# Loading a ring of expert weights in pairs: one 4 MB transfer and one semaphore for two 2 MB units in the middle rounds

## The chip, the cores and the metric

The kernel runs on one core of a Trainium2 chip. The metric is the device time of one execution in microseconds (us). All data are float32.

## The reference, cut to what matters

One decoder layer for 256 tokens of width 1024: two gated token mixers, then a mixture of 32 experts with four experts per token, then a final norm. The mixers, the router and the norms make up the first fifth of the time; the rest is the expert part:

```
def expert_block(args):
    xb, e = args
    gu = xb @ w_gu[e] + b_gu[e]                 # 1024 x 2048
    glu = jnp.minimum(gu[:, :D_FF], SWIGLU_LIMIT)
    lin = jnp.clip(gu[:, D_FF:], -SWIGLU_LIMIT, SWIGLU_LIMIT)
    act = glu * jax.nn.sigmoid(SWIGLU_ALPHA * glu) * (lin + 1.0)
    return act @ w_d[e] + b_d[e]                # 1024 x 1024
```

Each expert's weights (8 MB for gate and up, 4 MB for down) are read from HBM once. With 32 experts that is about 400 of the 432 MB that the kernel moves.

## The kernel before

**Items and rounds.** An *item* is one expert with up to 64 of its tokens; there are 32 items here. Two items (one even, one odd) make a *round*: 16 rounds, numbered 0 to 15. TensorE (PE) runs `item(j, odd)` once per item: four gate-up units, with the token gather, the turns and the scatter of neighbouring items between them, and the two down units of the item before.

**Units and the ring.** The weights come in *units* of 2 MB: 128 partitions with one row of 16 KB each. An expert has four gate-up units and two down units, a round has twelve. They land in the twelve slots of the tile `raw`. `ORDER` says which slot the unit at each *place* (0 to 11) of a round takes, so the loads and the matmuls walk over the slots in the same fixed order. Places 0 and 1 are gate-up units 2 and 3 of the even expert, 2 and 3 the down units of the odd expert before, 4 to 7 the four gate-up units of the odd expert, 8 and 9 the down units of the even expert, and 10 and 11 gate-up units 0 and 1 of the next round's even expert. The first two gate-up units of round 15's even item are thus loaded by round 14.

**Who waits for what.** All weight loads are issued by one queue, SyncE's (SP), in the order of use. PE raises the semaphore `used` by one when the last matmul of a unit is done. `load(k, ...)` waits until the unit that held its slot a round earlier is used, and issues one transfer (L531 for gate-up, L534 for down). A transfer adds 16 to its slot's semaphore, `raw_in[slot]`, when it has landed. Before the first matmul of a unit, PE waits in `landed_expert` for that semaphore. The matmuls of gate-up units are L1126, of down units L1149, of the last down units L1165; the turns are L668, the gather L1024, the scatter L1098 (L1087 in the last item).

**Three kinds of rounds.** Round 0's units are loaded by hand during the front part (`load_gate_up(0, 0, ORDER[0])` and so on), as slots come free from the mixers' weights, which lie in the same memory. Round 1 is the *opening* round: its places 0 to 5 are loaded in halves (`load_halves`). Rounds 2 to 14 are the SP loop `sp.Fori(2, pairs - 1)`, twelve single transfers a pass. Round 15 is the *last* round: places 0 to 6 singly, places 7 to 11 in two or four parts (`load_parts`), each with a semaphore of its own.

Of the kernel before, what the change touches and what calls it, by code (L numbers as in the profile page):

```python
# [47 lines left out]
GU_UNITS, DN_UNITS = 4, 2  # L48
UNITS = GU_UNITS + DN_UNITS
SLOTS_W = 2 * UNITS  # L50


HALVED = (0, 1, 2, 3, 4, 5)
# [2 lines left out]
PARTS = {7: 2, 8: 2, 9: 4, 10: 4, 11: 4}  # L56


ORDER = (6, 7, 1, 8, 2, 3, 4, 9, 10, 5, 0, 11)


Z_UNITS = [[(C_QI, 512)], [(C_KB, 128), (C_KI, HD + HEADS)], [(C_QB, 512)], [(0, C_QB)]]
# [95 lines left out]
def build(nc, x, head, positions, w_in, w_up,  # L158
# [4 lines left out]
    with ctx:  # L163
# [98 lines left out]
        raw = sb("raw", [P, SLOTS_W, UNIT])  # L262
# [128 lines left out]
        used = sem("used")  # L391
# [76 lines left out]
        def arrived(slot):  # L468
            return 16 * (FRONT_LOADS[slot] + (2 if slot == (U_WO + 1) % RING else 0))

        def landed_expert(eng, j, place):

            slot = ORDER[place % SLOTS_W]
            eng.wait_ge(raw_in[slot], 16 * j + (16 * (place // SLOTS_W + 1) + arrived(slot)))
            return raw[:, slot, :]

        def landed_part(eng, j, place, c):

            each = 4 // PARTS.get(place, 1)
            if c % each == 0 and c // each < PARTS.get(place, 1) - 1:  # L480
                eng.wait_ge(part_in[place][c // each], 16)
            elif c % each == 0:
                landed_expert(eng, j, place)

        def units_through_gate_up(i):

# [24 lines left out]
        def _(sp):  # L511
# [21 lines left out]
            def load_down(e, u, slot):  # L533
                sp.dma_start(raw[:, slot, :], w_dn_v[e, u]).then_inc(raw_in[slot], 16)  # L534
# [34 lines left out]
            load_gate_up(1, 2, ORDER[6])  # L569
            load_gate_up(1, 3, ORDER[7])  # L570
            sp.wait_ge(br_ok, 2 * KC)
            load_down(0, 0, ORDER[8])
            used_up(sp, 11)
            load_down(0, 1, ORDER[9])
            for q in range(2):
                sp.wait_ge(wo_ps, 4 + q)
                at = slice(q * UNIT // 2, (q + 1) * UNIT // 2)
# [4 lines left out]
            def load_round(j, last, opening=False):  # L582

                snap = (lambda e: e) if opening else sp.snap
                even = snap((2 * j) % EXPERTS)
                odd = snap((2 * j + 1) % EXPERTS)
                even_last = snap((2 * j + (EXPERTS - 1)) % EXPERTS)
                even_next = snap((2 * j + 2) % EXPERTS)

                def load(k, start, e, u):  # L590
                    sp.wait_ge(used, SLOTS_W * j + (k + 1 - SLOTS_W))
                    start(e, u, ORDER[k])

                def load_parts(k, src):
                    sp.wait_ge(used, SLOTS_W * j + (k + 1 - SLOTS_W))
                    n = PARTS.get(k, 1)
                    for c in range(n):
                        at = slice(c * UNIT // n, (c + 1) * UNIT // n)
                        done = part_in[k][c] if c < n - 1 else raw_in[ORDER[k]]
                        sp.dma_start(raw[:, ORDER[k], at], src(at)).then_inc(done, 16)  # L600

                def load_halves(k, src):

                    lead = UNIT // 4 if k == 0 else 0
                    if k == 0:
                        sp.wait_ge(quarter_used, 1)
                        sp.dma_start(raw[:, ORDER[k], 0:lead], src(slice(0, lead))).then_inc(half_in[k], 16)
                    sp.wait_ge(half_used, HALVED.index(k) + 1)
                    sp.dma_start(raw[:, ORDER[k], lead:UNIT // 2], src(slice(lead, UNIT // 2))).then_inc(half_in[k], 16)
                    sp.wait_ge(used, k + 1)  # L610
                    sp.dma_start(raw[:, ORDER[k], UNIT // 2:UNIT], src(slice(UNIT // 2, UNIT))).then_inc(raw_in[ORDER[k]], 16)

                def gate_up_of(e, u):
                    return lambda at: w_gu_v[e, u // 2, :, u % 2 * UNIT + at.start:u % 2 * UNIT + at.stop]

                if opening:
                    load_halves(0, gate_up_of(even, 2))
                    load_halves(1, gate_up_of(even, 3))
                    for u in range(DN_UNITS):
                        load_halves(2 + u, lambda at: w_dn_v[even_last, u, :, at])  # L620
                else:
                    load(0, load_gate_up, even, 2)
                    load(1, load_gate_up, even, 3)
                    for u in range(DN_UNITS):
                        load(2 + u, load_down, even_last, u)
                if last:
                    for u in range(GU_UNITS):
                        load_parts(4 + u, lambda at: w_gu_v[odd, u // 2, :, u % 2 * UNIT + at.start:u % 2 * UNIT + at.stop])
                    for u in range(DN_UNITS):
                        load_parts(8 + u, lambda at: w_dn_v[even, u, :, at])  # L630
                    for u in range(DN_UNITS):
                        load_parts(10 + u, lambda at: w_dn_v[odd, u, :, at])
                else:
                    for u in range(GU_UNITS):
                        if opening and 4 + u in HALVED:
                            load_halves(4 + u, gate_up_of(odd, u))
                        else:
                            load(4 + u, load_gate_up, odd, u)
                    for u in range(DN_UNITS):
                        load(8 + u, load_down, even, u)  # L640
                    for u in range(DN_UNITS):
                        load(10 + u, load_gate_up, even_next, u)

            load_round(1, False, True)
            sp.wait_ge(n_ok, 1)
# [15 lines left out]
        def _(pe):  # L661
# [437 lines left out]
                                       start=False, stop=True, skip_group_check=True)  # L1099
                    mm.then_inc(scat_ps, 1)  # L1100

            def gate_up(j, odd, u, parted=False):

                i = 2 * j + odd
                first = isinstance(i, int) and i == 0
                second = isinstance(i, int) and i == 1
                if first and u == 0:
                    pe.wait_ge(xT_half, 1)
                elif first and u == 1:
                    pe.wait_ge(xT_ok, 1)  # L1110
                elif u == 0:
                    pe.wait_ge(xT_ok, i + 1)
                    pe.wait_ge(bias_ok, 1 if second else 2 * i)
                place = u if first else UNITS * odd - DN_UNITS + u
                w = raw[:, ORDER[place % SLOTS_W], :] if parted else landed_expert(pe, j, place)
                last = u == GU_UNITS - 1
                for k in range(2):
                    b, c = u // 2, 2 * (u % 2) + k
                    for pair in range(2):
                        if parted:  # L1120
                            landed_part(pe, j, place, 2 * k + pair)
                        if second and u == 0 and k == 0 and pair == 1:
                            pe.wait_ge(bias_ok, 2)
                        for half in range(2):
                            at = k * 2 * FF + pair * FF + half * BLK
                            mm = pe.matmul(GU[pair][half * SLOTS:(half + 1) * SLOTS, :], xT[:, c, b, :],  # L1126
                                           w[:, at:at + BLK], start=u == 0 and k == 0, stop=last and k == 1)
                        if last and k == 1 and pair == 0:
                            mm.then_inc(glu_ps, 1)
                        if first and u == 0 and k == 0 and pair == 0:  # L1130
                            mm.then_inc(quarter_used, 1)
                    if place in HALVED and isinstance(i, int) and k == 0:
                        mm.then_inc(half_used, 1)
                mm.then_inc(used, 1)

            def down(j, odd, u, parted=False, chunks=range(4)):

                i = 2 * j + odd
                pe.wait_ge(act_ok, i + 1)
                if u == 0 and (not isinstance(i, int) or i > 0):  # L1140
                    pe.wait_ge(dn_ev, i)
                place = UNITS * odd + (UNITS + GU_UNITS - DN_UNITS) + u
                w = raw[:, ORDER[place % SLOTS_W], :] if parted else landed_expert(pe, j, place)
                for c in chunks:
                    if parted:
                        landed_part(pe, j, place, c)
# [82 lines left out]
            def item(j, odd, final=False):  # L1229

                i = 2 * j + odd
                gate_up(j, odd, 0)
                turn_scatter(i - 2)
                gate_up(j, odd, 1)
                scatter(i - 2)
                gate_up(j, odd, 2)
                if final:
                    pe.wait_ge(gain_in, 16)
                    spread_gain()
                gate_up(j, odd, 3)  # L1240
                if final:
                    pe.wait_ge(gain_ok, 2)
                next_tokens(i)
                down(j + (odd - 1), 1 - odd, 0)
                turn(i)
                turn_tokens(i + 1)
                down(j + (odd - 1), 1 - odd, 1)

            with pe.Fori(1, pairs - 1) as j:
                item(j, 0)  # L1250
# [757 lines left out]
```

## Time and profile before

| | us |
|---|---|
| median of three runs | 1104.85 |
| lowest and highest | 1104.22, 1108.11 |
| the profiled execution, its own time | 1105.68 |
| its span in the trace | 1103.9 |

The span runs from the first to the last instruction in the trace; the time of the same execution is 1.8 us longer. PE is busy for 97% of the span by the trace, and the 16 DMA engines move 392 GB/s as a mean over the span. The expert part begins at about 212 us. The last weights land at about 1094 us, and the output is stored by 1104 us.

### The profile page before, as it was taken

The numbers are of one execution on the slowest core, as the hardware profiler recorded it, in microseconds if no ns is written. First come the engines' busy times: TensorE is split into PE (matmuls) and PEld (weight loads), VectorE is DVE, ScalarE is ACT, GpSimd is POOL, SyncE is SP. The second block draws the span as 40 slices with busy tenths as digits, with TensorE's granted clock in tenths as the row PEclk, the third lists the DMA queues.
The fourth block names the chain that finished last, engine by engine and source line by source line (L and its number), as shares of the span: only waits on it lengthen the run. The fifth ranks groups of instructions, "written<-read, shape, count | busy, mean of one in ns | idle before, by whom it ended". The sixth has DMA issues, their size and how long they took to land.

```text
span 1103.9 us, 13223 instructions
## 1 busy us (share of the span) xinstructions
PE 1070.5 (97%) x5100; PEld 464.0 (42%) x5100; DVE 278.1 (25%) x653; ACT 168.3 (15%) x356; POOL 22.7 (2%) x45
## 2 busy tenths in 40 slices
PE   9999999999999999999999999999999999999997
PEld 6588785633333333333333333333333333233333
DVE  2086431332222222222222222222222111122122
ACT  2154430210001100100010000000000000000112
POOL 0221100000000000000000000000000000000000
PEclk9999999999999999999999999999999999999999
DMA  9935437899999999999999999999999999999996
GB/s 367 379 129 204 174 153 295 336 420 428 433 428 432 432 429 434 429 432 432 430 434 429 433 431 429 434 429 433 431 430 434 428 433 431 430 433 428 433 426 272
DMA packets 38372, 432.19 MB, mean 392 GB/s; under 512 B 4296, under 2 KB 6736, under 8 KB 12112
## 3 DMA queue, kind: packets, MB, share of 16 engines
q1 hardware_dynamic: 38208, 431.65, 92.5%
q8 instruction: 14, 0.23, 0.1%
q10 hardware_dynamic: 144, 0.26, 0.1%
q14 instruction: 6, 0.05, 0.0%
HBM read 430.84 MB, written 1.05 MB: 391 GB/s over the span
## 4 chain that ended last, share of the span: by engine, by line
PE 63%; SPq 24%; DMA 11%; issue 1%; DVE 1%; ACT 0%; another core or an unknown queue 0%; DVEq 0%; ACTq 0%
PE bank L1126 25%; SPq L531 12%; PE bank L1149 10%; DMA raw<-in_w_gate_up 9%; PE bank L664 8%; SPq L534 7%; SPq L600 5%; PE bank L668 4%; PE bank L691 4%; PE bank L1098 3%; PE bank L1024 3%; PE bank L942 2%; DMA raw<-in_w_down 2%; PE bank L949 1%; PE bank L744 1%
## 5 line engine op out<-in xcount | busy, mean ns | idle before, releaser
L1126 PE MATMUL bank<-raw,xT 128*64 128x512 f32 x2048 | 461.8, 597 | 23.8 <-DMA raw<-in_w_gate_up 22.9
L1126 PEld LDWEIGHTS bank<-raw,xT 128*64 128x64 f32 x2048 | 140.3, 137 | 315.7 <-issue 256.7
L1149 PE MATMUL bank<-raw,actT 128*64 128x512 f32 x992 | 225.0, 596 | 0.0
L1149 PEld LDWEIGHTS bank<-raw,actT 128*64 128x64 f32 x992 | 68.9, 137 | 127.3 <-issue 120.1
L1847 DVE TENSOR_TENSOR gub<-bank,bias_gu 128x512 f32<-128x512 f32 x64 | 43.9, 685 | 160.5 <-PE bank L668 160.4
L1795 DVE TENSOR_SCALAR gated<-cst,posc,gates 128x128 f32<-128x128 f32 x60 | 18.1, 343 | 261.1 <-PE bank L1098 261.1
L1854 DVE COPY ev_gu<-bank 128x512 f32<-128x512 f32 x32 | 22.1, 691 | 228.2 <-PE bank L1126 228.2
L1461 ACT COPY ev_gu<-bank 128x512 f32<-128x512 f32 x32 | 18.7, 585 | 361.7 <-PE bank L1126 361.7
L664 PE MATMUL bank<-hT,front_raw 128*128 128x256 f32 x256 | 58.6, 382 | 0.0
L1024 PE MATMUL bank<-x_res,onehot 128*64 128x512 f32 x248 | 58.5, 592 | 0.0
L1098 PE MATMUL bank<-ev,gated 64*128 64x512 f32 x232 | 57.6, 615 | 0.0
L664 PEld LDWEIGHTS bank<-hT,front_raw 128*128 128x128 f32 x256 | 47.5, 190 | 8.1 <-issue 2.1
L691 PE MATMUL bank<-front_raw,hT 128*128 128x512 f32 (+2 forms) x128 | 45.3, 514 | 0.5 <-DVE hT L1562 0.5
L668 PEld LDWEIGHTS bank<-cst,ev_gu 128*128 128x128 f32 x256 | 33.4, 210 | 25.2 <-issue 25.2
L1466 ACT ACTIVATE ev_gu<-gub 128x512 f32<-128x512 f32 x32 | 20.1, 629 | 153.1 <-DVE gub L1861 153.1
L668 PE MATMUL bank<-cst,ev_gu 128*128 128x128 f32 x256 | 39.4, 297 | 0.0
L1098 PEld LDWEIGHTS bank<-ev,gated 64*128 64x128 f32 x232 | 20.0, 186 | 37.2 <-issue 37.2
L1024 PEld LDWEIGHTS bank<-x_res,onehot 128*64 128x64 f32 x248 | 17.9, 137 | 35.3 <-issue 35.3
L691 PEld LDWEIGHTS bank<-front_raw,hT 128*128 128x128 f32 x128 | 23.8, 193 | 20.7 <-issue 19.9
L1471 ACT COPY ev<-bank 128x512 f32<-128x512 f32 x31 | 18.1, 585 | 81.4 <-PE bank L1149 81.4
L1440 ACT COPY ev<-bank 128x512 f32<-128x512 f32 x31 | 18.1, 585 | 72.6 <-PE bank L1024 72.6
L1883 DVE TENSOR_TENSOR actT<-gub,ev_gu 128x512 f32<-128x512 f32 x31 | 21.4, 692 | 24.0 <-PE bank L1149 23.9
(267 smaller groups left out, 594.6 us busy)
## 6 DMA issues: line engine op xcount, KB each, us to landing
raw<-in_w_gate_up SPq DMA_DIRECT2D x122, 2048.0 KB, 43.5
raw<-in_w_down SPq DMA_DIRECT2D x58, 2048.0 KB, 44.1
raw<-in_w_gate_up SPq DMA_DIRECT2D x11, 1024.0 KB, 7.6
front_raw<-in_w_in SPq DMA_DIRECT2D x5, 2048.0 KB, 22.4
raw<-in_w_down SPq DMA_DIRECT2D x6, 1024.0 KB, 9.1
raw<-in_w_down SPq DMA_DIRECT2D x12, 512.0 KB, 18.7
front_raw<-in_w_branch_mla SPq DMA_DIRECT2D x1, 2048.0 KB, 7.7
front_raw<-in_w_branch_dsa SPq DMA_DIRECT2D x1, 2048.0 KB, 7.7
```

The source lines that it names most:

```text
L531: sp.dma_start(raw[:, slot, :], w_gu_v[e, u // 2, :, u % 2 * UNIT:(u % 2 + 1) * UNIT]).then_inc(raw_in[slot], 16)
L534: sp.dma_start(raw[:, slot, :], w_dn_v[e, u]).then_inc(raw_in[slot], 16)
L600: sp.dma_start(raw[:, ORDER[k], at], src(at)).then_inc(done, 16)
L664: mm = pe.matmul(o, lhs(c), rhs(c), start=start and c == 0, stop=c == n - 1)
L668: return pe.transpose(o, src, ident)
L691: return pe.matmul(ZB[t][:, 0:w], hT[:, c, t * P:(t + 1) * P], z_weight(n, c), start=c == 0, stop=c == KC - 1)
L1024: mm = pe.matmul(PREP[half * SLOTS:(half + 1) * SLOTS, :], onehot[:, t, :], xs[:, t, half * BLK:(half + 1) * BLK], start=t == 0, stop=t == ...
L1098: mm = pe.matmul(ACC[2 * t + half][:, :], scat[rows, t * P:(t + 1) * P], ev[rows, :], start=False, stop=True, skip_group_check=True)
L1126: mm = pe.matmul(GU[pair][half * SLOTS:(half + 1) * SLOTS, :], xT[:, c, b, :], w[:, at:at + BLK], start=u == 0 and k == 0, stop=last and k ...
L1149: mm = pe.matmul(DN[half * SLOTS:(half + 1) * SLOTS, :], actT[:, c, u, :], w[:, at:at + BLK], start=u == 0 and c == 0, stop=u == DN_UNITS ...
L1847: dve.tensor_tensor(gub[:, pair, :].rearrange("p (j s) -> p j s", s=SLOTS), GU[pair][:, :].rearrange("p (j s) -> p j s", s=SLOTS), bias_gu ...
L1854: dve.tensor_copy(ev_gu[:, 1, :], GU[1][:, :]).then_inc(lin_ev, 1)
```

## The change

In rounds 2 to 14 two neighbouring places are loaded by one transfer of 4 MB, `load_pair`. It waits until both slots are free, it moves both units, and it signals only the semaphore of the first slot. PE waits for that semaphore before the first unit of the pair; before the second one it waits for a constant that is reached long before. In the opening round places 10 and 11 are loaded that way as well. The last round is loaded as before; its waits count one more load on the slots whose semaphore the pairs did not raise (`final`).

A transfer walks its two slots by a positive step, so places 8 and 9 exchange their slots (10, 5 become 5, 10). In the front part the two down units of item 0 are therefore issued in the other order: the second one at once, the first after the wait for its slot.

```diff
-ORDER = (6, 7, 1, 8, 2, 3, 4, 9, 10, 5, 0, 11)
+ORDER = (6, 7, 1, 8, 2, 3, 4, 9, 5, 10, 0, 11)
...
-        def landed_expert(eng, j, place):
+        def landed_expert(eng, j, place, final=False):
 
-            slot = ORDER[place % SLOTS_W]
-            eng.wait_ge(raw_in[slot], 16 * j + (16 * (place // SLOTS_W + 1) + arrived(slot)))
+            k = place % SLOTS_W
+            slot = ORDER[k]
+            alone = 1 if k == SLOTS_W - 1 else 2
+            if k % 2 == 0:
+                eng.wait_ge(raw_in[slot], 16 * j + (16 * (place // SLOTS_W + 1) + arrived(slot)))
+            elif isinstance(j, int) and j + place // SLOTS_W == 0:
+                eng.wait_ge(raw_in[slot], 16 + arrived(slot))
+            else:
+                eng.wait_ge(raw_in[slot], 16 * (alone + 1 if final and place >= 0 else alone) + arrived(slot))
             return raw[:, slot, :]
...
             sp.wait_ge(br_ok, 2 * KC)
+            load_down(0, 1, ORDER[9])
+            used_up(sp, 11)
             load_down(0, 0, ORDER[8])
-            used_up(sp, 11)
-            load_down(0, 1, ORDER[9])
...
+                def load_pair(k, src):
+                    sp.wait_ge(used, SLOTS_W * j + (k + 2 - SLOTS_W))
+                    a, b = ORDER[k], ORDER[k + 1]
+                    sp.dma_start(raw[:, a:b + 1:b - a, :], src).then_inc(raw_in[a], 16)
+
+                def gate_up_pair(e, b):
+                    return w_gu_v[e, b].rearrange("p (s n) -> p s n", s=2)
+
+                def down_pair(e):
+                    return w_dn_v[e].rearrange("b p n -> p b n")
...
-                else:
+                elif last:
                     load(0, load_gate_up, even, 2)
                     load(1, load_gate_up, even, 3)
                     for u in range(DN_UNITS):
                         load(2 + u, load_down, even_last, u)
+                else:
+                    load_pair(0, gate_up_pair(even, 1))
+                    load_pair(2, down_pair(even_last))
...
+                else:
+                    load_pair(4, gate_up_pair(odd, 0))
+                    load_pair(6, gate_up_pair(odd, 1))
+                    load_pair(8, down_pair(even))
+                    load_pair(10, gate_up_pair(even_next, 0))
```

On SP, the loop body of before (rounds 2 to 14) begins with these rows; `ISA [waits used]` is the wait on the semaphore, the DMA row behind it the transfer with its partitions and elements per partition, and the register row works out the next wait's value:

```order
L531 ISA [waits used]
L531 DMA raw<-in_w_gate_up 128x4096
L591 REGISTER_ALU
L531 ISA [waits used]
L531 DMA raw<-in_w_gate_up 128x4096
L591 REGISTER_ALU
L534 ISA [waits used]
L534 DMA raw<-in_w_down 128x4096
L591 REGISTER_ALU
L534 ISA [waits used]
L534 DMA raw<-in_w_down 128x4096
```

The same places 0 to 3 in the loop body of the changed kernel, and behind them places 4 to 7:

```order
L604 ISA [waits used]
L604 DMA raw<-in_w_gate_up 128x8192
L602 REGISTER_ALU
L604 ISA [waits used]
L604 DMA raw<-in_w_down 128x2x4096
L602 REGISTER_ALU
L604 ISA [waits used]
L604 DMA raw<-in_w_gate_up 128x8192
L602 REGISTER_ALU
L604 ISA [waits used]
L604 DMA raw<-in_w_gate_up 128x2x4096
```

Twelve waits and transfers of a pass have become six. Where the two slots are neighbours and the source is contiguous (places 0 and 1, places 4 and 5) a partition gets one row of 8192 elements, 32 KB; the four other pairs have two pieces of 16 KB per partition.

On PE, the head of item 30 in the changed kernel (the first item of round 15, whose first two units are loaded by round 14) reads as follows; before, the same rows stood there with other line numbers:

```order
L1151 MATMUL bank<-raw,xT 64x512 [waits raw_in0]
L1151 MATMUL bank<-raw,xT 64x512 x7
L1087 REGISTER_ALU
L693 MATMUL bank<-cst,gated 128x128 [waits gated_ok]
L693 MATMUL bank<-cst,gated 128x128
L1151 MATMUL bank<-raw,xT 64x512 [waits raw_in11]
L1151 MATMUL bank<-raw,xT 64x512 x7
```

No PE instruction has moved here. What differs is what raises `raw_in0`, for which the first unit waits: before it was that unit's own 2 MB, now it is the 4 MB of both units. The value asked of `raw_in11` has long been reached by then.

## Rows read from the trace of the kernel before

**Rows 1.** The page's slices (40 equal ones): GB/s moved; and its DMA issues.
```profile
GB/s 367 379 129 204 174 153 295 336 420 428 433 428 432 432 429 434 429 432 432 430 434 429 433 431 429 434 429 433 431 430 434 428 433 431 430 433 428 433 426 272
...
raw<-in_w_gate_up SPq DMA_DIRECT2D x122, 2048.0 KB, 43.5
```

**Rows 2.** Two stretches: busy us (count) of five engines, clock, DMA share, GB/s.
```profile
300.00:700.00 400.00, 400.00 (x1890) 143.97 (x1888) 88.03 (x180) 40.90 (x75) 0.00 (x0) 1.00 1.01 431
760.00:1030.00 270.00, 252.02 (x1172) 88.03 (x1168) 56.53 (x115) 25.74 (x47) 0.00 (x0) 1.00 1.01 431
```

**Rows 3.** Timeline of PE, three stretches: start, us, instructions, idle before.
```profile
254.60 3.60 PE L1126 MATMUL bank<-raw,xT 128*64 128x512 f32 x16
...
258.50 3.65 PE L1126 MATMUL bank<-raw,xT 128*64 128x512 f32 x16
...
709.33 3.65 PE L1126 MATMUL bank<-raw,xT 128*64 128x512 f32 x16 [0.56 <-DMA raw<-in_w_gate_up]
...
1030.22 3.65 PE L1126 MATMUL bank<-raw,xT 128*64 128x512 f32 x16 [0.56 <-DMA raw<-in_w_gate_up]
...
1035.07 3.65 PE L1126 MATMUL bank<-raw,xT 128*64 128x512 f32 x16 [0.83 <-DMA raw<-in_w_gate_up]
1038.66 1.99 PE L1098 MATMUL bank<-ev,gated 64*128 64x512 f32 x8
1040.57 3.65 PE L1126 MATMUL bank<-raw,xT 128*64 128x512 f32 x16
```

**Rows 4.** Groups of PE by line in the stretch 1040 to 1103.9 us.
```profile
L1126 PE MATMUL bank<-raw,xT 128*64 128x512 f32 x96 | 21.7, 597 | 0.0
L1149 PE MATMUL bank<-raw,actT 128*64 128x512 f32 x64 | 14.5, 596 | 0.0
L1165 PE MATMUL bank<-raw,xT 128*64 128x256 f32 x64 | 7.8, 385 | 0.3 <-DMA raw<-in_w_down 0.2
```

**Rows 5.** Timeline of PE at the end, 1085 to 1095 us.
```profile
1085.25 2.29 PE L1165 MATMUL bank<-raw,xT 128*64 128x256 f32 x16 [0.15 <-DMA raw<-in_w_down]
...
1089.39 5.59 PE L1165 MATMUL bank<-raw,xT 128*64 128x256 f32 x48
```

**Rows 6.** Last round: transfer of place 6, second half of place 8; issue to landing.
```profile
L600 SPq DMA_DIRECT2D raw<-in_w_gate_up x1: 5814/5814/5814, 1018.4 to 1018.4; - x1
DMA to landing us min/median/max: 50.7/50.7/50.7
...
L600 SPq DMA_DIRECT2D raw<-in_w_down x1: 4068/4068/4068, 1040.2 to 1040.2; - x1
DMA to landing us min/median/max: 38.7/38.7/38.7
```

**Rows 7.** Opening round, SP: place 9 issued and landing; place 11 issued.
```profile
L534 SPq DMA_DIRECT2D raw<-in_w_down x1: 328/328/328, 254.8 to 254.8; - x1
DMA to landing us min/median/max: 12.1/12.1/12.1
...
L531 SPq DMA_DIRECT2D raw<-in_w_gate_up x1: 328/328/328, 262.2 to 262.2; - x1
```

**Rows 8.** Single 2 MB transfers into an empty queue: one row, four pieces per partition.
```profile
L531 SPq DMA_DIRECT2D raw<-in_w_gate_up x1: 340/340/340, 122.6 to 122.6; - x1
DMA to landing us min/median/max: 7.2/7.2/7.2
...
L523 SPq DMA_DIRECT2D front_raw<-in_w_branch_dsa x1: 379/379/379, 75.6 to 75.6; - x1
DMA to landing us min/median/max: 7.7/7.7/7.7
```

**Rows 9.** Front: second down unit of item 0 issued; first matmul on down units.
```profile
L534 SPq DMA_DIRECT2D raw<-in_w_down x1: 328/328/328, 186.5 to 186.5; - x1
DMA to landing us min/median/max: 12.9/12.9/12.9
...
245.91 3.63 PE L1149 MATMUL bank<-raw,actT 128*64 128x512 f32 x16
```

More of the change, by code:

```diff
@@ L482, in landed_part @@
             elif c % each == 0:
-                landed_expert(eng, j, place)
+                landed_expert(eng, j, place, True)
         def units_through_gate_up(i):
@@ L632, in load_round @@
                         load_parts(10 + u, lambda at: w_dn_v[odd, u, :, at])
-                else:
+                elif opening:
                     for u in range(GU_UNITS):
-                        if opening and 4 + u in HALVED:
+                        if 4 + u in HALVED:
                             load_halves(4 + u, gate_up_of(odd, u))
@@ L640, in load_round @@
                         load(8 + u, load_down, even, u)
-                    for u in range(DN_UNITS):
-                        load(10 + u, load_gate_up, even_next, u)
+                    load_pair(10, gate_up_pair(even_next, 0))
[3 more added lines that the diff above has]
+                    load_pair(8, down_pair(even))
+                    load_pair(10, gate_up_pair(even_next, 0))
             load_round(1, False, True)
@@ L1100, in scatter, with gate_up @@
                     mm.then_inc(scat_ps, 1)
-            def gate_up(j, odd, u, parted=False):
+            def gate_up(j, odd, u, parted=False, final=False):
                 i = 2 * j + odd
@@ L1114, in gate_up @@
                 place = u if first else UNITS * odd - DN_UNITS + u
-                w = raw[:, ORDER[place % SLOTS_W], :] if parted else landed_expert(pe, j, place)
+                w = raw[:, ORDER[place % SLOTS_W], :] if parted else landed_expert(pe, j, place, final)
                 last = u == GU_UNITS - 1
@@ L1134, in gate_up, with down @@
                 mm.then_inc(used, 1)
-            def down(j, odd, u, parted=False, chunks=range(4)):
+            def down(j, odd, u, parted=False, chunks=range(4), final=False):
                 i = 2 * j + odd
@@ L1142, in down @@
                 place = UNITS * odd + (UNITS + GU_UNITS - DN_UNITS) + u
-                w = raw[:, ORDER[place % SLOTS_W], :] if parted else landed_expert(pe, j, place)
+                w = raw[:, ORDER[place % SLOTS_W], :] if parted else landed_expert(pe, j, place, final)
                 for c in chunks:
@@ L1231, in item @@
                 i = 2 * j + odd
-                gate_up(j, odd, 0)
+                gate_up(j, odd, 0, final=final)
                 turn_scatter(i - 2)
-                gate_up(j, odd, 1)
+                gate_up(j, odd, 1, final=final)
                 scatter(i - 2)
-                gate_up(j, odd, 2)
+                gate_up(j, odd, 2, final=final)
                 if final:
@@ L1239, in item @@
                     spread_gain()
-                gate_up(j, odd, 3)
+                gate_up(j, odd, 3, final=final)
                 if final:
@@ L1243, in item @@
                 next_tokens(i)
-                down(j + (odd - 1), 1 - odd, 0)
+                down(j + (odd - 1), 1 - odd, 0, final=final)
                 turn(i)
                 turn_tokens(i + 1)
-                down(j + (odd - 1), 1 - odd, 1)
+                down(j + (odd - 1), 1 - odd, 1, final=final)
             with pe.Fori(1, pairs - 1) as j:
```

## The prediction

> **What bounds the kernel now.** I read the DMA line of the page first. From about 250 us to the end it holds 428 to 434 GB/s [rows 1], and the two stretches cut out of the loop both give 431 GB/s, one with PE busy for all of its 400 us and one with PE idle for 18 of 270 us [rows 2]. So the transfer stream runs without a gap through the whole expert part, whatever PE does. At 431 GB/s a unit of 2.097 MB takes 4.87 us, a round of twelve 58.4 us.
>
> The second look is at PE's timeline. Up to 709.33 us it never waits for weights; it lives on the stock in the ring. That row carries the first wait for a transfer [rows 3]. From there on the stream sets the pace: at 1030.22 and at 1035.07 us PE starts the first two units of item 30 right as they land, after 0.56 and 0.83 us of idle time [rows 3]. These two units are the last that round 14 loads, and under the change they are one pair.
>
> The third look decides the sum: what PE does from there to the end. The groups of the stretch from 1040 us show no idle time before the gate-up and down units (0.0) and 0.3 us before the last down units [rows 4]. The chip's last transfers and PE's last matmuls are tied: PE waits 0.15 us at 1085.25 us [rows 5], and else it is busy. So the last 60 us are a chain of PE work that begins when the last unit of round 14 lands, with hardly any slack in it.
>
> **The change part by part.**
>
> *The last pair lands as one.* This is the main term. The stream is not disturbed, so the pair is complete when its second half was before, at 1035.0 us. PE then starts the first unit at 1035.07 us where it started the second. Without a wait the second follows 258.50 - 254.60 = 3.90 us later [rows 3], and 0.05 more for the start out of idle (3.65 against 3.60 us for the same sixteen matmuls): 1039.02 instead of 1035.07 us. PE is 3.95 us late. The bounds are 3.9 and 4.1.
>
> *What the rest gives back.* Lateness is absorbed only where PE waits for something that does not move with it. That is the 0.15 us at 1085.25 us, and what is hidden inside the two groups of L1165: 48 matmuls take 5.59 us, so 0.11 us each behind the first one's 0.38, and sixteen would take 2.05; they take 2.29 [rows 5]. A further 0.1 us may hide at the very last part. Together 0.5 us, between 0.3 and 0.7. The groups between give nothing back [rows 4]. The weights of round 15 are no new wait: the next unit's matmuls ran from 1040.57 us without idle time [rows 3], and everything behind has 3.95 us more time to land.
>
> *The pairs before that one.* In the stretch bound by the stream a pair arrives every 9.73 us. The longest work between two pairs is that of gate-up units 0 and 1, with the turn and the scatter: 3.95 us plus 1040.57 - 1035.07 = 5.50 us, 9.45 us [rows 3]. PE is ready before each pair lands, so lateness does not add up from pair to pair. PE runs into the data earlier, since a pair's first unit lands 4.87 us later; the time is not longer for it, as the waits come out of the stock that PE would have used up later.
>
> *The issue side.* Slots come back in pairs, so a pair is issued when its second slot is free. From issue to landing a unit has 43.5 us as a median [rows 1] and up to 50.7 [rows 6]; a pair issued some 5 us later than its first half was leaves the stream at least four pairs. The tight place is the first pair, at places 10 and 11 of the opening round. It is issued at 262.2 us; the transfer ahead of it lands at 254.8 + 12.1 = 266.9 us [rows 7]. A transfer into an empty queue lands after 7.2 us [rows 8], of which 4.87 are its bytes, so 2.3 us are set-up and completion. The pair comes 4.7 us ahead, 2.4 us more than it needs. Cost nothing; if setting up 4 MB took twice as long, still next to nothing (0 to 0.3 us).
>
> *The rate of the stream.* 79 pairs take the place of 158 transfers (thirteen rounds by six, and one). No row of before shows a 4 MB transfer. The nearest comparison is with halves: from the landing of place 6 at 1069.1 us to that of the second half of place 8 at 1078.9 us, four transfers of 1 MB take 9.8 us [rows 6], 4.90 us for 2 MB against 4.87. If the 0.035 us are the price of the shorter row (8 instead of 16 KB per partition), only the 26 pairs with rows of 32 KB gain, 0.017 us for each of 52 units: 0.9 us. If they are the price of one more transfer, all 79 pairs gain, 2.7 us. If a 32 KB row is cut in the chip, nothing. I take 0.4 us, between nothing and the price of the row, and keep 0 and 2.7 for the range.
>
> *Edits at no cost.* The exchange of two slots in the front part delays the first down unit of item 0 by one transfer, to 186.5 + 12.9 = 199.4 us; it is first used at 245.91 us [rows 9], 46 us later. If that cover were gone it would cost 4.87 us. The six waits and registers that SP saves per pass lie in a queue that is 40 us ahead.
>
> Sum: 3.95 - 0.5 - 0.4 = +3.05 us. The profiled execution took 1105.68 us (span 1103.9), so a profiled one should come to about 1108.7. It was 0.8 us above the median of the three; on the median of 1104.85 the sum gives 1107.9 us, 0.3% slower. A measurement here can tell about 0.5% (5.5 us) from no change, so that is within it.
>
> **A page against the row.** The Trainium skill, page "DMA: Bandwidth & Descriptors", section "Anatomy of one DMA", gives a transfer about 2.0 us of fixed cost beside its bytes at 436 GB/s (fitted for transfers that GpSimd issues). If that were paid one after the other, 79 transfers fewer would save 158 us, and the sum would be 950 us. The trace disagrees for this queue: by that estimate a 2 MB transfer alone would run at 308 GB/s, and the stream runs at 431 [rows 2].
>
> **The rivals.**
>
> *A. Transfers in two pieces per partition run slower, and it ends more than 0.5% slower.* 53 of the pairs have two pieces per partition, from two places in HBM or to two slots. The nearest row is a 2 MB load with four pieces of 4 KB: 7.7 against 7.2 us [rows 8], 0.5 us for three more pieces, 0.17 a piece. If each of the 53 pays 0.1 us the stream ends 5.3 us later, and the whole comes to 3.45 + 5.3 = +8.8 us, 1113.6; at 0.17 to +12.4 us, 1117.3. Against it: those pieces are four times smaller, and a set-up cost is hidden by 40 us of queue. It decides from (5.5 - 3.45) / 53 = 0.04 us per such pair. Chance 0.14.
>
> *B. The price per transfer is real.* Then 2.7 us come back, as worked out above: 3.95 - 0.5 - 2.7 = +0.75 us, 1105.6. The halves speak for it, the rows of 8 KB explain them as well. Chance 0.14.
>
> *C. The stream speeds up beyond that, or PE's lateness is made good, and it ends faster by over 0.5%.* That needs 9 us, 0.057 us per unit, more than halving ever cost. The same page, section "Where 436 GB/s comes from", puts the ceiling at 435 GB/s; an estimate from it is 4.82 us for a unit, so that 158 units could gain 7 us at most. Chance 0.04.
>
> *D. The stream starves in rounds 1 to 3 because pairs are issued later.* It needs a set-up more than 2.4 us longer than that of a single transfer, and each 1 us above that costs 1 us at the first pairs. Against it speaks the issue itself, 0.33 us. Priced at 1 to 3 us it would give 1109 to 1111. Chance 0.03.
>
> **How the numbers follow.** My forecast (a loss of 2 to 5 us) has 0.65. The range reaches down to B's time with a little for the measurement, 1104.5, and up to between the forecast and A, 1112; A's upper part and C stay outside. Faster by over 0.5% is C, 0.04; slower by over 0.5% is A and the end of D, 0.15; the rest is 0.81.
>
> **What would show it.** In the trace after: a loop at 431 GB/s again; PE's waits for transfers beginning about one round earlier (near 655 us instead of 709), three for each item as now; item 30's first unit starting at about 1035 and its second at 1039 us; then no idle time to the end and no wait at the last down units; the last transfer landing near 1094 us as before, and a span near 1107. Rates above 433 GB/s in the loop would mean B, below 429 A. A DMA share that dips between 260 and 300 us would mean D. I am wrong in the main step if item 30's second unit starts at 1039 us and the end does not move with it.

## The result and the profile after

| | median us | lowest, highest | runs |
|---|---|---|---|
| before | 1105.36 | 1104.22, 1108.11 | 18 |
| changed | 1107.56 | 1106.64, 1109.77 | 18 |

The ratio is 1.0017, 95% interval 1.0011 to 1.0024: the changed kernel is 2.2 us slower (1.2 to 2.7 by the interval). The forecast was 3.05 us slower, within 0.5%. The profiled execution of the changed kernel took 1109.63 us, 2.1 us above its own median, with a span of 1107.8 us. A second series (experiment 5) gave 1108.6 against 1105.02 us, ratio 1.0032 (1.0019 to 1.0045). So the medians say 2.2 and 3.6 us slower, and the two intervals together reach from 1.2 to 5.0 us.

The page after: its slices, two groups of PE over the whole span, and the pair transfers (the first and the last answer to [rows 1]):

```profile
GB/s 363 365 128 202 190 152 285 336 418 415 432 424 440 427 435 430 435 427 435 431 431 434 432 431 438 427 437 427 438 428 432 433 431 435 427 439 427 430 426 232
...
L1151 PE MATMUL bank<-raw,xT 128*64 128x512 f32 x2048 | 459.3, 596 | 14.0 <-DMA raw<-in_w_gate_up 12.8
...
L1174 PE MATMUL bank<-raw,actT 128*64 128x512 f32 x992 | 225.7, 596 | 12.5 <-DMA raw<-in_w_down 12.5
...
raw<-in_w_gate_up SPq DMA_DIRECT2D x53, 4096.0 KB, 46.7
```

The stream is as full as before. In the loop of before PE's waits for weights stood only before gate-up units; now half of them (12.5 us) stand before the down units, since each pair is waited for at its first unit.

PE's timeline after, at the first wait, at the last pair and at the end (it answers to [rows 3] and [rows 5]; the line numbers are 25 higher):

```profile
657.45 3.65 PE L1151 MATMUL bank<-raw,xT 128*64 128x512 f32 x16 [0.86 <-DMA raw<-in_w_gate_up]
...
1026.35 3.65 PE L1174 MATMUL bank<-raw,actT 128*64 128x512 f32 x16 [0.97 <-DMA raw<-in_w_down]
...
1035.97 3.65 PE L1151 MATMUL bank<-raw,xT 128*64 128x512 f32 x16 [0.75 <-DMA raw<-in_w_gate_up]
...
1039.92 3.65 PE L1151 MATMUL bank<-raw,xT 128*64 128x512 f32 x16
...
1089.79 1.90 PE L1190 MATMUL bank<-raw,xT 128*64 128x256 f32 x16
...
1093.53 5.40 PE L1190 MATMUL bank<-raw,xT 128*64 128x256 f32 x48
```

The first wait comes at 657 us (before: 709). Item 30's first unit starts when its pair is complete, at 1035.97 us, and its second follows without a wait, 3.95 us later. At the last down units no wait is left: sixteen matmuls take 1.90 us where they took 2.29, and 48 take 5.40 for 5.59. The last weights land at 1096.1 us and not near 1094: 0.9 us of that is the last pair's, and 1.5 us is one gap of 6.4 us between two landings (1055.4 and 1061.8 us). PE, 4.85 us later than before at item 30's second unit, does not wait for them.

The opening of the loop holds what was not forecast. First the groups of the changed kernel's first pair and the transfer ahead of it (issue and landing, as [rows 7]), then two stretches of each trace by window (columns as [rows 2]), before and after:

```profile
L541 SPq DMA_DIRECT2D raw<-in_w_down x1: 328/328/328, 256.1 to 256.1; - x1
DMA to landing us min/median/max: 11.1/11.1/11.1
...
L604 SPq DMA_DIRECT2D raw<-in_w_gate_up x1: 674/674/674, 263.5 to 263.5; - x1
DMA to landing us min/median/max: 15.4/15.4/15.4
```

```profile
264.00:268.00 4.00, 4.00 (x22) 1.42 (x22) 0.60 (x2) 0.00 (x0) 0.00 (x0) 1.00 0.98 422
...
262.00:290.00 28.00, 28.00 (x134) 10.31 (x134) 5.87 (x12) 2.76 (x5) 0.00 (x0) 1.00 1.01 430
```

```profile
264.00:268.00 4.00, 4.00 (x22) 1.29 (x20) 0.60 (x2) 0.00 (x0) 0.00 (x0) 1.00 0.96 352
...
262.00:290.00 28.00, 28.00 (x134) 9.88 (x130) 5.87 (x12) 2.76 (x5) 0.00 (x0) 1.00 0.99 411
```

The pair is complete at 278.9 us, 11.7 us behind the landing at 267.2 us, where two units take 9.7. For 4 us the stream moves 352 instead of 422 GB/s. By the landings that is 2.0 us lost. By the bytes moved from 262 to 290 us (411 against 430 GB/s over 28 us) it is 1.2 us; the rest of the later landing is not explained.

Later the stream is faster than before. Issue and landing of the changed kernel's pair at places 10 and 11 in rounds 2 and 14:

```profile
L604 SPq DMA_DIRECT2D raw<-in_w_gate_up x1: 548/548/548, 317.1 to 317.1; - x1
DMA to landing us min/median/max: 20.0/20.0/20.0
...
L604 SPq DMA_DIRECT2D raw<-in_w_gate_up x1: 549/549/549, 985.6 to 985.6; - x1
DMA to landing us min/median/max: 50.3/50.3/50.3
```

From 337.1 to 1035.9 us are 698.8 us for twelve rounds, 58.23 each. Before, the unit at place 11 was issued at 315.7 and 985.5 us in these rounds and landed 19.1 and 49.5 us later: from 334.8 to 1035.0 us, 58.35 each. The gain is 0.11 to 0.12 us a round, 1.4 us over the thirteen.

### The profile page after: what moved, and what is told of

The parts are those of the page before. It is cut to its first block, busy times and chain, and to the rows that moved or that the text cites. A ratio compares the mean times of both kernels' runs of the same rounds, so it can differ in the third digit from the quotient of the medians.

```text
span 1107.8 us, 12910 instructions
## 1 busy us (share of the span) xinstructions
PE 1071.9 (97%) x5100; PEld 465.3 (42%) x5100; DVE 278.2 (25%) x653; ACT 168.4 (15%) x356; POOL 22.7 (2%) x45
## 4 chain that ended last, share of the span: by engine, by line
PE 67%; DMA 31%; DVE 1%; issue 0%; ACT 0%; another core or an unknown queue 0%; SPq 0%; DVEq 0%; ACTq 0%
DMA raw<-in_w_down 31%; PE bank L1151 23%; PE bank L1174 15%; PE bank L689 8%; PE bank L693 5%; PE bank L716 4%; PE bank L1049 3%; PE bank L1123 3%; PE bank L967 2%; PE bank L974 1%; PE bank L1190 1%; PE bank L769 1%; PE bank L755 1%; PE bank L1112 0%; DMA front_raw<-in_head 0%; PE bank L987 0%
## 5 line engine op out<-in xcount | busy, mean ns | idle before, releaser
L1174 PE MATMUL bank<-raw,actT 128*64 128x512 f32 x992 | 225.7, 596 | 12.5 <-DMA raw<-in_w_down 12.5
L1174 PEld LDWEIGHTS bank<-raw,actT 128*64 128x64 f32 x992 | 68.9, 137 | 142.7 <-issue 127.5
## 6 DMA issues: line engine op xcount, KB each, us to landing
raw<-in_w_gate_up SPq DMA_DIRECT2D x16, 2048.0 KB, 11.7
```

Of the source, the lines that this page charges most:

```text
L1174: mm = pe.matmul(DN[half * SLOTS:(half + 1) * SLOTS, :], actT[:, c, u, :], w[:, at:at + BLK], start=u == 0 and c == 0, stop=u == DN_UNITS ...
```

## The experiments

All changes are against the kernel named, and the code shown is cut. Eight kernels of the layer were timed in two series (1 to 4, 5 to 8), 5 to 12 executions each; within a series they share the executions of before. There is one trace of each. The two kernels of transfers alone were run once each.

**1. The kernel before, PE waits for both units of the last pair.** Transfers are untouched.

```diff
+            landed_expert(pe, pairs - 1, -1)
             item(pairs - 1, 0, True)
```

> The kernel before with one wait more: ahead of item 30's first unit PE also waits for its second unit. All transfers stay single. Theory (the loss of the change is PE's late start at the last pair): PE's second unit starts 3.9 to 4.0 us later, 0.9 us come back at the last down units, so 3.05 us over before, about 1108.4 us, with the stream landing as before (last weights near 1094 us). Rival (the loss lies in the stream of transfers, PE's lateness is made good on the way): within 1 us of before.

Measured: 1110.6 us, ratio 1.0045 (1.0022 to 1.0067), 5.3 us over before and not 3.05. The timeline shows why, and then the window of these matmuls in this run and in before:

```profile
1034.85 5.76 PE L1126 MATMUL bank<-raw,xT 128*64 128x512 f32 x16 [5.69 <-DMA raw<-in_w_gate_up]
...
1040.91 3.65 PE L1126 MATMUL bank<-raw,xT 128*64 128x512 f32 x16
```

```profile
1034.00:1041.00 7.00, 6.15 (x20) 1.85 (x22) 0.00 (x0) 0.00 (x0) 0.00 (x0) 0.63 1.02 435
```

```profile
1034.00:1041.00 7.00, 6.17 (x28) 1.95 (x29) 0.16 (x1) 0.37 (x1) 0.00 (x0) 1.00 1.02 435
```

PE had caught up, so that it idled for 5.69 us before the pair, and was then granted 0.63 of its clock over those 7 us (part of them at the lower of its two levels, 1.2 GHz) where before it had 1.00. The second unit starts 6.06 us after the first and not 3.95. Take those 2.1 us off and 3.2 us are left, near the theory's 3.05. The stream ended as in before (last weights at 1093.4 us). The rival is out, but the run has a cost of its own in it, so experiment 8 repeats it without that.

**2. The changed kernel, round 14 loaded singly too.** The last pair is then twelve units ahead of item 30's second unit.

```diff
-            with sp.Fori(2, pairs - 1) as j:
+            with sp.Fori(2, pairs - 2) as j:
                 load_round(j, False)
+            load_round(pairs - 2, False, single=True)
...
-            with pe.Fori(1, pairs - 1) as j:
+            with pe.Fori(1, pairs - 2) as j:
...
+            item(pairs - 2, 0, 1)
+            item(pairs - 2, 1, 1)
+            item(pairs - 1, 0, 2)
```

> The changed kernel with round 14 loaded singly too (pairs in rounds 2 to 13 and in the opening round's last two places). Theory: PE catches up in the twelve single units by 0.4 us each, 4.9 us in all, so nothing of the late start is left at the end: 3.05 us less than the changed kernel, about 1104.5 us, item 30's first unit again starting one transfer ahead of its second. Rival (the loss lies in the stream): as the changed kernel, 1107.6 us.

Measured: 1105.79 us, ratio to before 0.9996 (0.9976 to 1.0017). PE's timeline at item 30 is that of before again:

```profile
1030.84 3.65 PE L1159 MATMUL bank<-raw,xT 128*64 128x512 f32 x16
...
1035.66 3.65 PE L1159 MATMUL bank<-raw,xT 128*64 128x512 f32 x16 [0.80 <-DMA raw<-in_w_gate_up]
```

The first unit runs while the second is under way, and the second starts at its landing. With the pairs of all other rounds in place the slowdown is gone within the interval; it lay in how the last pair of the run meets the unpaired tail. The time is 1.8 us below the changed kernel's and 1.3 us above what was expected. In its trace the first two pairs land 11.1 and 11.3 us behind the landings ahead of them, where two units take 9.7: 2.9 us lost in the opening of the loop, against 2.0 in the changed kernel's trace.

**3. The changed kernel, places 10 and 11 of the opening round loaded singly.**

```diff
-                    load_pair(10, gate_up_pair(even_next, 0))
+                    for u in range(DN_UNITS):
+                        load(10 + u, load_gate_up, even_next, u)
```

> The changed kernel with places 10 and 11 of the opening round loaded singly. Theory (a 4 MB transfer is set up for longer than a 2 MB one, and the first pair comes too late for it: in the changed kernel's trace it lands 11.7 us after the transfer ahead of it and not 9.7): the gap goes back to 9.7 us unless the next pair takes it over, and 0.8 to 2 us are saved, 1105.6 to 1106.8 us. Rival (the gap is only a matter of which engine is last and costs nothing at the end): 1107.6 us.

Measured: 1107.6 us, ratio 1.0011 (0.999 to 1.0033): nothing is saved. By the trace the next pairs take the gap over. Issue and landing of opening place 11, then of the last pair of round 2:

```profile
L538 SPq DMA_DIRECT2D raw<-in_w_gate_up x1: 328/328/328, 261.4 to 261.4; - x1
DMA to landing us min/median/max: 13.4/13.4/13.4
...
L604 SPq DMA_DIRECT2D raw<-in_w_gate_up x1: 555/555/555, 315.0 to 315.0; - x1
DMA to landing us min/median/max: 20.8/20.8/20.8
```

From 274.9 to 335.9 us twelve units take 61.0 us, where before took 58.3: 2.7 us lost. It is lost at four of the six pairs, 0.3 to 0.9 us each, and two of these four were issued 8 and 10 us ahead of the landing before them. So a short queue does not explain all of it. Experiment 6 loads in the same way up to here and loses nothing.

**4. The kernel before, single transfers issued two by two.** `late` holds in every round but the last, and `k_late` is 10 in the opening round and else 0.

```diff
-                    sp.wait_ge(used, SLOTS_W * j + (k + 1 - SLOTS_W))
+                    if late and k >= k_late:
+                        if k % 2 == 0:
+                            sp.wait_ge(used, SLOTS_W * j + (k + 2 - SLOTS_W))
+                    else:
+                        sp.wait_ge(used, SLOTS_W * j + (k + 1 - SLOTS_W))
```

> The kernel before with its single transfers issued two by two, each pair when its second slot is free (opening places 10 and 11, rounds 2 to 14). Every transfer keeps its 2 MB and its semaphore. Theory (the gap at the first pair comes from the size of the transfer, not from the late issue): no gap over 4.95 us between landings in 260 to 300 us and the time of before, 1105.4 us. Rival (it comes from the late issue): the landings of opening places 10 and 11 come 1 to 2 us late, and so does the end, 1106.4 to 1107.4 us.

Measured: 1106.3 us, ratio 1.0007 (0.9986 to 1.0028), by the time unclear between the two. In the trace the stretch 264 to 268 us moves 393 GB/s, between before's 422 and the changed kernel's 352:

```profile
264.00:268.00 4.00, 4.00 (x22) 1.40 (x20) 0.41 (x2) 0.00 (x0) 0.00 (x0) 1.00 0.97 393
```

No landing from 260 to 300 us comes more than 5.1 us behind the one ahead of it. Opening place 11 lands 9.9 us behind place 9 (before: 9.7), not 1 to 2 us late, and to the end of round 14 the landings slip by 0.4 us. So the late issue alone costs 0.2 us at this place, a small part of the early loss.

**5. The changed kernel once more, unchanged.**

> The changed kernel once more, unchanged, for a second trace beside those below: 1107.4 us within 0.7. In rounds 3 to 14 twelve units again land in 58.24 us (58.35 for single transfers); theory (the slow landings of the first pairs are a loss that depends on how far the queue is ahead): the landings of rounds 1 and 2 again take 1 to 2 us more than with single transfers; rival (they were an accident of one trace): no more than before.

Measured: 1108.6 us, ratio 1.0032 (1.0019 to 1.0045). It is 1.2 us above the expected 1107.4, outside its 0.7. Twelve units again land in 58.24 us in rounds 3 to 14. The early loss is there again: the transfer ahead of the first pair lands at 265.5 us, the pair at 276.9, 11.4 us behind it. The stretch 264 to 268 us again moves 352 GB/s. This trace ends 1.9 us earlier than the first, as its last pair lands at 1034.0 us instead of 1035.9.

**6. Pairs only in rounds 2 to 13** (experiments 2 and 3 together).

> Pairs only in rounds 2 to 13: places 10 and 11 of the opening round and all of round 14 singly. Theory: nothing of PE's late start is left, rate 1.3 us better over twelve rounds, but 1 to 2 us lost in round 2, where pairs still come while the queue is short: 1105.0 to 1106.0 us, the same as the kernel before within 0.7. Rival (the first pair alone was the loss in the stream): 1104.0 us.

Measured: 1105.91 us, ratio 1.0006 (0.9997 to 1.0015), the time that the theory had. But the trace does not show the loss that the theory got it from. Opening place 11 and the last pair of round 2, as in experiment 3:

```profile
L538 SPq DMA_DIRECT2D raw<-in_w_gate_up x1: 328/328/328, 262.3 to 262.3; - x1
DMA to landing us min/median/max: 14.3/14.3/14.3
...
L604 SPq DMA_DIRECT2D raw<-in_w_gate_up x1: 560/560/560, 315.9 to 315.9; - x1
DMA to landing us min/median/max: 19.0/19.0/19.0
```

Round 2 takes 58.3 us (276.6 to 334.9), as before, though its first pairs are issued only 5.2 and 4.7 us ahead of the landing before them. What this trace loses, it loses at the end: a gap of 6.2 us between two landings of round 15, and PE starts the last down units 1.2 us later behind item 30's second unit than in before (1085.54 - 1034.14 = 51.40 us against 50.18). The hit of the theory's time is in part luck. The rival's 1104.0 us is out as a time; its mechanism (only the first pair loses) fits this trace and not that of experiment 3.

**7. Pairs only in rounds 6 to 13.**

> Pairs only in rounds 6 to 13, where transfers are issued 30 us and more ahead; single transfers in all other rounds. Theory (a pair costs only at a short queue and only at the end): no loss in the early rounds, none at the end, and 0.11 us gained in each of eight rounds: 0.9 us below the kernel before, 1104.4 us, and 3 us below the changed kernel. Rival (pairs cost something wherever they are): 1105.5 us or more.

Measured: 1104.97 us against 1105.02, ratio 1.0005 (0.9996 to 1.0013). The early rounds, all single here, move 431 GB/s from 262 to 290 us; in the rounds of pairs twelve units land in 58.24 us and not 58.35, which is the 0.9 us expected; the last unit of round 14 lands at 1033.3 us. But in the time nothing of it shows. In the trace it is lost again: 0.4 us in round 2 (single transfers), 0.2 us in round 14, and 0.8 us at one gap of 5.6 us between two landings of round 15, behind which PE waits for the last down units (0.24 us at 1084.27 us). The time is 3.6 us below the changed kernel of its series and equal to before: no version beats before.

**8. The kernel before, PE waits for both units at every pair of places.** All transfers are single and issued as before.

```diff
+            if not isinstance(j, int) and place % 2 == 0 and not (closing[0] and place >= 0):
+                landed_expert(eng, j, place + 1)
```

> The kernel before, every transfer single and issued as before; only PE waits before the first unit of each pair of places for both units (to the last pair of round 14). Theory: PE's idle times are then those of the changed kernel, at most 1.1 us each, its clock stays up (in the run in which it waited for the last pair alone it idled for 5.7 us and the next sixteen matmuls took 5.76 instead of 3.65 us), so the pure price of landing as one shows: 3.95 - 0.9 = 3.05 us, 1108.4 us. Rival (the changed kernel's loss comes mostly from its stream): under 1107 us.

Measured: 1108.18 us against 1105.02, 3.2 us slower, ratio 1.003 (1.0018 to 1.0042). Its timeline at the last pair and its group of the last down units:

```profile
1034.41 3.65 PE L1130 MATMUL bank<-raw,xT 128*64 128x512 f32 x16 [0.68 <-DMA raw<-in_w_gate_up]
...
1038.36 3.65 PE L1130 MATMUL bank<-raw,xT 128*64 128x512 f32 x16
```

```profile
L1169 PE MATMUL bank<-raw,xT 128*64 128x256 f32 x64 | 7.3, 381 | 0.0
```

This is the change's waiting alone, without one larger transfer, and it costs what the whole change costs.

**9. Transfers alone.** The forms of the ring, nothing of the layer is computed.

> A kernel that only moves weights through the ring's slots, with the kernel's transfer forms, and computes nothing of the layer: three times each form into an empty queue; four times each form (and as a reference two single transfers) issued when one 2 MB transfer is still under way; then trains, 60 single transfers, 30 pairs with 32 KB rows, 30 gate-up pairs in two pieces, 30 down pairs. Theory (a pair is set up more slowly, but streams with less loss per byte): into the empty queue a pair takes over 12.1 us (7.2 + 4.87), by some us; behind one 2 MB transfer it lands 1 to 2 us later than two single transfers; the trains land a single in 4.86 us and a pair in 9.71 us or a little less. If the length of the rows were the cause of the better rate, only the 32 KB rows would be under 9.72 us; if the number of transfers, all three pair forms alike. Rival (pairs are set up as quickly): 12.1 us into the empty queue and no difference behind a transfer.

Issue and landing of a single, a pair with 32 KB rows and a pair in two pieces, each into an empty queue:

```profile
L29 SPq DMA_DIRECT2D raw<-in_w_gate_up x1: 385/385/385, 0.7 to 0.7; - x1
...
DMA to landing us min/median/max: 7.2/7.2/7.2
...
L33 SPq DMA_DIRECT2D raw<-in_w_gate_up x1: 333/333/333, 7.9 to 7.9; - x1
DMA to landing us min/median/max: 12.0/12.0/12.0
...
L37 SPq DMA_DIRECT2D raw<-in_w_gate_up x1: 552/552/552, 64.5 to 64.5; - x1
DMA to landing us min/median/max: 12.6/12.6/12.6
```

The trains of singles, 32 KB pairs, two-piece gate-up pairs and down pairs, by window (clock, DMA share, GB/s at the end):

```profile
500.00:760.00 260.00, 0.00 (x0) 1.00 1.01 429
810.00:1060.00 250.00, 0.00 (x0) 1.00 1.00 432
1110.00:1340.00 230.00, 0.00 (x0) 1.00 1.01 429
1400.00:1640.00 240.00, 0.00 (x0) 1.00 1.01 428
```

A pair into the empty queue takes 12.0 to 12.7 us, so its set-up is at most 0.7 us longer than a single's (7.2 + 4.9 = 12.1). Behind one 2 MB transfer, issued 4.9 us ahead of its landing, it lands in time. Here are that transfer and the pair:

```profile
L29 SPq DMA_DIRECT2D raw<-in_w_gate_up x1: 434/434/434, 155.9 to 155.9; - x1
DMA to landing us min/median/max: 11.7/11.7/11.7
...
L37 SPq DMA_DIRECT2D raw<-in_w_gate_up x1: 552/552/552, 162.8 to 162.8; - x1
DMA to landing us min/median/max: 14.6/14.6/14.6
```

The pair lands 9.8 us behind the transfer ahead of it (177.4 against 167.6), and so do two single ones at the same lead in the four repeats (9.8 us). The theory of a slow set-up is refuted. The trains settle the rate: only the 32 KB rows run faster, 432 GB/s against 428 to 429. A pair in two pieces gains nothing over two singles, so the number of transfers is not what costs. What the rate follows is the length of the rows. The Trainium skill, page "DMA: Bandwidth & Descriptors", section "Anatomy of one DMA", says (for transfers that GpSimd issues) that a transfer's fixed cost is mostly the wait for the last byte's receipt. By these trains that wait is no occupation of the queue: halving the number of transfers left 429 GB/s as it was.

**10. How late may a pair be issued?** Transfers alone again.

> Transfers alone again, nothing of the layer is computed: four quarters of 512 KB, then, when one, two, three or all four of them have landed, 4 MB, once as a pair in two pieces and once as two single transfers, four times each. In the kernel with pairs the pair of the opening round was issued 3.7 us ahead of the landing before it and landed 11.7 us after it, in place of 9.8. Theory (a pair needs 12.7 us from issue to landing, so it is late when it is issued less than 2.9 us ahead, and its lateness then shows whole, while of two single transfers only the first need be ready, 7.2 - 4.9 = 2.3 us): with 3.7 us of lead both land 9.8 us behind the last quarter; at 2.5 us the pair 10.2 and the singles 9.8; at 1.2 us 11.4 and 10.9; with none 12.7 and 12.1. Rival (a pair at a short queue loses some 2 us more than that): 11.7 us already at 3.7 us of lead.

Four quarters of 512 KB go first. The pair is issued at 4.5 us, behind a last quarter issued at 2.1; the two singles at 22.6 and 23.0 us, behind a last quarter issued at 20.3. Issue to landing of the pair's last quarter, of the pair and of the second single:

```profile
L50 SPq DMA_DIRECT2D raw<-in_w_gate_up x1: 432/432/432, 2.1 to 2.1; - x1
DMA to landing us min/median/max: 6.2/6.2/6.2
...
L37 SPq DMA_DIRECT2D raw<-in_w_gate_up x1: 650/650/650, 4.5 to 4.5; - x1
DMA to landing us min/median/max: 14.5/14.5/14.5
...
L29 SPq DMA_DIRECT2D raw<-in_w_gate_up x1: 432/432/432, 23.0 to 23.0; - x1
DMA to landing us min/median/max: 13.2/13.2/13.2
```

Issued 3.8 us ahead of the last quarter's landing, the pair lands 10.7 us behind it (19.0 against 8.3), the two singles 9.8 us (36.2 against 26.5, before rounding 9.79). At 2.5 us of lead both land 10.0 to 10.4 us behind, at 1.2 us 11.5 and 10.9, at none 12.6 and 12.1. (The four repeats gave 10.7 to 11.1 us for the pair at 3.8 us of lead and 9.7 to 9.8 for the singles.) Neither had it fully: at the lead that the kernel has, a pair in two pieces loses 0.9 to 1.3 us where two singles lose nothing, but not the 1.4 to 2.0 us that the first pair loses in the kernel's traces. Nor does the loss grow as the lead shrinks: the pair is later at 3.8 us of lead than at 2.5.

## Why the prediction was right, point by point

**What bounds the kernel** held. The stream sets the pace from the stock's end on, PE's chain sets the end. The end is the landing of round 14's last unit plus a constant: 1103.9 - 1035.0 = 68.9 us before, 1107.8 - 1035.9 = 71.9 and 1105.9 - 1034.0 = 71.9 us in the two traces of the change. The traces of experiments 2 and 4 have 68.9 us as well, those of 3 and 8 71.9 and 72.0. Three are off it: experiment 1 (74.3, by the lost clock) and experiments 6 and 7 (70.0 and 69.5, where weights of round 15 came late). The difference of 3.0 us is the price of landing as one. Experiment 8 has it as a time, 3.2 us, and experiment 2 takes it away. The stream's slices hold 428 to 434 GB/s only up to the last two, which have 426 and 272; nothing in the sum hangs on that.

**The last pair lands as one, 3.95 us.** Right: 1039.92 - 1035.97 = 3.95 us.

**What the rest gives back, 0.5 us.** Mis-sized: 0.9 us, outside the stated 0.3 to 0.7. The second unit is 4.85 us later than in before, the end 3.95 us. The last down units begin 1085.25 - 1035.07 = 50.18 us after item 30's second unit in before and 1089.79 - 1039.92 = 49.87 us after it now, 0.3 us, of which the row of before showed 0.15; inside the two groups 2.29 - 1.90 = 0.4 and 5.59 - 5.40 = 0.2 us were hidden. I had worked out the hidden part from the rate of the second group, which had a hidden wait of its own.

**The pairs before that one** held: PE waits 0.75 to 0.97 us before the pairs shown, at most 1.1 us before any, and nothing adds up.

**The issue side, cost nothing,** failed as a step. I took the lead over the landing in the trace of before, 4.7 us. In the changed kernel it was 3.7 us, as the pair was issued at 263.5 instead of 262.2 us and the landing ahead of it came at 267.2 instead of 266.9, and at that lead the pair landed late: 2.0 us in this trace, 1.7 us in the second, 1.4 us in that of experiment 2. The term that I put at nothing (0 to 0.3 us) is 1.4 to 2.0 us. This is rival D, which I gave 0.03, with its sign: the DMA share from 262 to 290 us is 0.99 for 1.01. Its price was right, its condition (a set-up 2.4 us longer) was not: the set-up is the same within 0.7 us (experiment 9). A pair behind a short queue is worth 0.9 to 1.3 us (experiment 10), the late issue 0.2 us (experiment 4). The later pairs of round 2 lose from nothing (experiments 5 and 6) to 2.7 us (experiment 3) at leads of 4 to 10 us, and single transfers can lose as well: the trace of experiment 1 has one gap of 6.2 us between landings at 304.0 and 310.2 us, 1.3 us too long. So part of the early loss comes and goes from trace to trace.

**The rate of the stream, 0.4 us.** Mis-sized: 1.4 us. By the price of the row length I had 0.9 us for 26 pairs with 32 KB rows, and took less since I could not tell whether such a row stays whole. That the row length is the mechanism is shown by the trains alone, where such a pair takes 9.71 us and the others 9.79, 0.16 us a round by two such pairs; the kernel gains 0.11, and its landings do not tell the two forms apart. Rival B, the price per transfer, is refuted by the two-piece trains, and so is A: two pieces per partition stream as fast as singles.

The two errors in the stream, +1.4 to +2.0 and -1.0 us, and the one in what the end gives back, -0.4, nearly cancel. So the main term was understood, and that the sum of 3.05 us lies between 2.2 and 3.6 with three of its small terms wrong is in part luck.

**What stays open:** why the first pair loses 1.4 to 2.0 us in the kernel where transfers alone lose 0.9 to 1.3 us at the same lead; why the pairs behind it lose up to 2.7 us in one trace and nothing in another; what makes the gaps of 5.6 to 6.4 us between landings in round 15, which three of the six traces with pairs have and none of the four without; and why PE reaches the loop up to 2 us sooner or later from trace to trace. With one trace of most kernels no run separates these.

## What to carry to other kernels

A larger transfer with one semaphore does not only save issues: its first half becomes usable when its second half lands. Where a stream of loads bounds the kernel that is free in the middle, since the consumer waits anyway. It costs once, at the last such load ahead of a tail that has no slack: the consumer's work on the first half (3.95 us here; the half's transfer takes 4.87), less what the tail can give back (0.9 us). So return to small pieces as many units before the end as the consumer needs to catch up (here it gains 0.4 us of 4.9 per unit; twelve units were enough, fewer were not tried). Before merging transfers for speed, ask whether the queue was ever short: in the full queue of the trains halving the number of transfers changed nothing, and only longer rows moved the rate (by 0.8%). And a single trace is no measure of 1 us here: landings slipped by 1 to 3 us in some traces and not in others of the same loads.

## What the runs showed of the hardware that I had not expected

- After 5.69 us of idle time PE was granted 0.63 of its clock from 1034 to 1041 us of experiment 1 (sixteen matmuls in 5.76 instead of 3.65 us); idle times of up to 1.2 us left it at 1.00 (experiment 8).
- A 4 MB transfer into an empty queue lands after 12.0 to 12.7 us. One in two pieces, issued 3.8 us ahead of the landing before it, takes 14.4 to 14.9 us and lands 0.9 to 1.3 us later than two single ones; issued 4.9 us ahead it loses nothing (experiments 9 and 10).
- Rows of 32 KB stream at 432 GB/s where rows of 16 KB stream at 428 to 429, whether in 2 MB or in 4 MB transfers (experiment 9).
